# mLSTM heads: the sample part of the denominators read ahead of unit 4's update, the prompt part behind the sums of squares

## What is computed

```
den = inter * einsum('bhtk,bhk->bht', qc, n) + sum(S, axis=-1)
h = num / maximum(abs(den), exp(-m_t))[..., None]
C_new = scale * C + einsum('bhsk,bhsv->bhkv', kw, vc)
n_new = scale * n + sum(kw, axis=2)
...
h = h * rsqrt(mean(h * h, axis=-1) + EPS)
```

## Time and profile before

| what | us |
|---|---|
| median of 3 runs | 1970.97 |
| lowest and highest | 1969.07, 1975.01 |
| the profiled execution | 1968.61 |
| its span | 1966.9 |
| PE busy | 1897.9 (96%) |
| DVE busy | 714.5 (36%) |
| ACT busy | 720.9 (37%) |
| POOL busy | 820.2 (42%) |

### The profile page before, as it was taken

One profiled execution on the slowest core, in us unless ns is written; L12 is line 12 of the kernel. 1 busy time (PEld: TensorE's weight loads), 2 busy tenths in 40 slices (PEclk: granted clock), 3 DMA queues, 4 the chain that ended last, 5 costly groups with the idle time before them and its releaser, 6 DMA issues.

```text
span 1966.9 us, 35914 instructions
## 1 busy us (share of the span) xinstructions
PE 1897.9 (96%) x13701; PEld 1755.9 (89%) x13701; DVE 714.5 (36%) x844; ACT 720.9 (37%) x1054; POOL 820.2 (42%) x683
## 2 busy tenths in 40 slices
PE   6999999999999999899999999999999999999997
PEld 6999999999999999898554654999999999999996
DVE  5687742111111122576756567222121111111213
ACT  3567743322222235434432432432443322222342
POOL 4242564453544544563110100543655535534442
PEclk7999999999999999999999999999999999999998
DMA  3232232223222223322478578322222222222222
GB/s 108 82 86 76 80 105 75 86 81 85 81 80 85 80 81 74 79 86 86 162 240 301 191 243 281 120 82 73 82 87 83 83 82 84 80 83 78 86 75 70
DMA packets 187147, 209.70 MB, mean 107 GB/s; under 512 B 24475, under 2 KB 150051, under 8 KB 186991
## 3 DMA queue, kind: packets, MB, share of 16 engines
q1 hardware_dynamic: 186394, 207.67, 33.8%
q10 hardware_dynamic: 648, 0.59, 0.1%
HBM read 167.57 MB, written 40.64 MB: 106 GB/s over the span
## 4 chain that ended last, share of the span: by engine, by line
PE 81%; issue 6%; DVE 5%; POOL 4%; ACT 3%; DMA 1%; ACTq 0%; POOLq 0%; DVEq 0%
PE ps L2145 68%; POOL W_LO L641 2%; PE ps L2434 2%; PE ps L2471 2%; PE ps L2373 2%; PE ps L2412 1%; POOL SQUARE_SUM L649 1%; PE ps L2489 1%; PE ps L2307 1%; PE ps L2422 1%; DVE H_PAD L1664 1%; DVE C_HALVES L1956 1%; DVE K_T L1827 1%; PE ps L2445 0%; DMA ML_IN_ROWS<-in_state_mlstm_conv_dram 0%
## 5 line engine op out<-in xcount | busy, mean ns | idle before, releaser
L641 POOL TENSOR_TENSOR W_LO<-W_RAW,W_HI 128x512 fp32r<-128x512 f32 x464 | 611.3, 1327 | 664.7 <-ACT W_HI L956 664.4
L956 ACT ACTIVATE W_HI<-W_RAW 128x512 fp32r<-128x512 f32 x484 | 297.8, 628 | 704.3 <-PE ps L2145 698.4
L2145 PE MATMUL ps<-A_HI,W_HI 128*128 128x288 f32 x2304 | 497.2, 298 | 15.1 <-POOL W_LO L641 6.6
L2145 PE MATMUL ps<-A_LO,W_HI 128*128 128x288 f32 x2304 | 494.7, 296 | 0.0
L2145 PE MATMUL ps<-A_HI,W_LO 128*128 128x288 f32 x2304 | 494.4, 296 | 0.0
L2145 PEld LDWEIGHTS ps<-A_HI,W_HI 128*128 128x128 f32 x2304 | 373.0, 190 | 18.0 <-issue 13.9
L2145 PEld LDWEIGHTS ps<-A_LO,W_HI 128*128 128x128 f32 x2304 | 373.0, 190 | 0.0
L2145 PEld LDWEIGHTS ps<-A_HI,W_LO 128*128 128x128 f32 x2304 | 372.6, 189 | 0.0
L2145 PE MATMUL ps<-G_HI,W_HI 128*128 128x288 f32 x768 | 164.7, 296 | 0.5 <-DVEq L1742 0.5
L2145 PE MATMUL ps<-G_LO,W_HI 128*128 128x288 f32 x768 | 164.5, 296 | 0.0
L2145 PE MATMUL ps<-G_HI,W_LO 128*128 128x288 f32 x768 | 164.4, 296 | 0.0
(11 more groups left out here) (368 smaller groups left out, 2333.2 us busy)
## 6 DMA issues: line engine op xcount, KB each, us to landing
W_RAW<-in_ffn_w_up_dram SPq DMA_DIRECT2D x176, 256.0 KB, 2.8
C_HALVES<-in_state_mlstm_C_dram SPq DMA_DIRECT2D x64, 512.0 KB, 4.9
out_ml_C_s_dram<-C_HALVES SPq DMA_DIRECT2D x64, 512.0 KB, 5.2
W_RAW<-in_ffn_w_down_dram SPq DMA_DIRECT2D x88, 256.0 KB, 2.7
W_RAW<-in_ml_w_in_dram SPq DMA_DIRECT2D x64, 256.0 KB, 2.8
W_RAW<-in_rg_w_in_dram SPq DMA_DIRECT2D x48, 256.0 KB, 2.8
W_RAW<-in_ple_w_gate_dram SPq DMA_DIRECT2D x32, 256.0 KB, 2.7
W_RAW<-in_ml_w_out_dram SPq DMA_DIRECT2D x32, 256.0 KB, 2.8
```

The costliest lines, as they stand in the source:

```text
L641: pool.tensor_tensor(W_LO[:, s], W_RAW[:, s], W_HI[:, s].bitcast(F32), ALU.subtract).then_inc(lo_ready, 1)
L956: act.activation(W_HI[:, s], W_RAW[:, s], ACT.Copy).then_inc(hi_ready, 1)
L2145: ins = pe.matmul(ps[:, 4 * s + 2 * m + h, 0:HALF_T], a[:, w, k, wc], x[:, h * HALF_T:h * HALF_T + HALF_T], start=i == 0 and k == 0 and q ...
```

## The change

`denominators` is split in two functions. The samples' part is called between update 3 and update 4, and the prompt's part where `denominators` was, behind `add_squares`. Each function waits at its end for its own last instruction. No instruction is added, left out or altered.

```diff
-            def denominators(h):
-
-                bank = at(h, "den")
-                if h == 0:
-                    dve.wait_ge(rows_spread, 16)
-                dve.wait_ge(piece_done, DONE[h, "den"])
-                link(dve.scalar_tensor_tensor(DEN[:, 0:SEQ], ps[:, bank, :], -1.0, EXP_NEG_M[:, 0:SEQ], ALU.mult, ALU.max))
-                dve.tensor_tensor(DEN[:, 0:SEQ], ps[:, bank, :], DEN[:, 0:SEQ], ALU.max).then_inc(bank_freed[bank], 1)
-                dbank, bank = bank, at(h, "ds")
+            def sample_denominators(h):
+
+                bank = at(h, "ds")
                 dve.wait_ge(piece_done, DONE[h, "ds"])
                 link(dve.scalar_tensor_tensor(DEN[:, SEQ:T], ps[:, bank, 0:N_STOK], -1.0, rows_of[h % 2][:, 1, :], ALU.mult, ALU.max))
                 dve.tensor_tensor(DEN[:, SEQ:T], ps[:, bank, 0:N_STOK], DEN[:, SEQ:T], ALU.max)
...
                 dve.wait_ge(bank_freed[bank], FREED[h, "ds", bank])
-                dve.wait_ge(bank_freed[dbank], FREED[h, "den", dbank])
+
+            def prompt_denominators(h):
+
+                bank = at(h, "den")
+                if h == 0:
+                    dve.wait_ge(rows_spread, 16)
+                dve.wait_ge(piece_done, DONE[h, "den"])
+                link(dve.scalar_tensor_tensor(DEN[:, 0:SEQ], ps[:, bank, :], -1.0, EXP_NEG_M[:, 0:SEQ], ALU.mult, ALU.max))
+                dve.tensor_tensor(DEN[:, 0:SEQ], ps[:, bank, :], DEN[:, 0:SEQ], ALU.max).then_inc(bank_freed[bank], 1)
+                dve.wait_ge(bank_freed[bank], FREED[h, "den", bank])
...
                 update(h, 3)
+                sample_denominators(h)
                 update(h, 4)
                 add_squares(h, Q_T[:, :, 0:SEQ], squares_p, sums_p)
-                denominators(h)
+                prompt_denominators(h)
                 update(h, 5)
```

## The result

The changed kernel is slower: a median of 1979.2 us over 20 runs, against 1969.03 us of the kernel before over 20 runs, a ratio of 1.0045 (95% interval 1.0025 to 1.0064). The forecast was 1961.5 us, in a range of 1956 to 1967. What strikes first is the spread. The kernel before ran from 1965.6 to 1975.5 us, the changed one from 1961.8 to 1988.7. Its two fastest executions, both 1961.8 us, are where the forecast was; half of all are above 1979. The profiled execution took 1979.06 us.

What follows compares the result with a forecast made beforehand. PE was taken as the bound, with `cp1` waiting 1.9 us a head for line 1989 and then running at half clock. 3.58 us a head, cut by load landings to 9.4 in all, gave 1961.5 us, range 1956.0 to 1967.0.

Steps and rivals of the forecast that it cites:

- The gain of head 3: End of head 3: its 3.1 us pass into the first slab's wait, as the last stores move with unit 7.
- the landings: Ahead of unit 7: it starts when its last half-unit load lands, limiting the gain to 1.5, 2.1, 2.7 and 3.1 us.
- These loads don't come earlier: Sample-state loads for unit 7: held by a chain of stores from updates 3 and 4, with DMA engines full.
- the sum: Four heads' gains, old start of unit 7 less its load's landing: 9.4 us off the span and the median.
- What hangs on the new wait: PE at unit 7: waits 0.5 to 2.1 us; clock loss taken as zero, upper bound 1.61 us a head.
- Rival 4: Behind unit 7: clock falls and stays down; with 8 us of half clock a head, 1977.6 us; chance 0.04.
- Rival 2: At unit 7: clock falls there instead, giving back 6.4 us, 1968.0 us (1964.8 in two heads only); chance 0.14.
- Rivals 1: Ahead of unit 7: loads don't hold it, transfers may pack better; gain 14.3 us, 1956.7 us; chance 0.14.
- 3: Change from head 3 to the slabs: head 3's gain lost, last stores held in queue; 1964.7 us; chance 0.14.
- 5: At `cp1`: a second condition nearly as late, so the change frees nothing; 1971 us; chance 0.04.

Runs made afterwards that it cites:

- e11: The changed kernel itself, run once more beside others on the same chip: 1982.0 us median of 12, ratio 1.0053 to the kernel before.
- e1: The kernel before with two added ScalarE copies of cp2, making PE idle about 1.9 us ahead of unit 7: 2018.8 us, ratio 1.0214.
- e8: The kernel before with one added ScalarE copy of cp2, a wait of about 1.3 us ahead of unit 7: 1975.2 us, ratio 1.0042.
- e4: The changed kernel with cp3's matmuls in one run behind cn and the samples' numerators behind them: 1962.6 us, ratio 0.9964.
- e7: The changed kernel with cn moved ahead of unit 7, cp3 in one run behind unit 7, then the numerators: 1966.3 us, ratio 0.9971.
- e3: The changed kernel with the first two of cp3's four row blocks moved ahead of unit 7, into its wait: 1964.2 us, ratio 0.997.
- e10: The changed kernel with cn and cp3's first row block moved ahead of unit 7, the rest in turns with numerators: 1958.8 us, ratio 0.9944.
- e12: The changed kernel with cp3's first row block moved ahead of unit 7 and cn left behind it: 1973.9 us, ratio 1.0026.
- e6: The kernel before with cp3 in one run behind cn, then the numerators, and no wait added: 1977.7 us, ratio 1.004.

## Why the prediction was wrong

*What held.* The samples' part fits DVE's idle time, update 4 keeps its place, and `cp1` starts behind unit 5 at full clock, as worked out (3.70 us). PE then waits for a load ahead of unit 7, as worked out, 0.5 to 1.9 us a head; it also waits 0.2 to 0.7 us ahead of unit 6, which the prediction did not have. The gain of head 3 passed into the slabs: PE's wait there is 3.21 us, as it was in the earlier trace rows, though the half clock behind it lasted longer, which costs 1.7 us.

*The first term that was mis-sized: the landings.* "These loads don't come earlier" was right; that they come no later was an unsaid part of the sum. Line 530 for half 15 of heads 1 and 2 after, to be read against the earlier trace rows:

```profile
L530 SPq DMA_DIRECT2D C_HALVES<-in_state_mlstm_C_dram x1: 380/380/380, 1067.8 to 1067.8; - x1
DMA to landing us min/median/max: 5.8/5.8/5.8
...
L530 SPq DMA_DIRECT2D C_HALVES<-in_state_mlstm_C_dram x1: 380/380/380, 1151.8 to 1151.8; - x1
DMA to landing us min/median/max: 5.5/5.5/5.5
```

Counted from each head's unit 4 (1055.35 and 1139.34), they land after 18.2 and 18.0 us; before it was 17.6 and 17.0. Unit 7 came 1.7, 1.3, 1.6 and 2.3 us earlier in the four heads, 6.9 us together where the sum had 9.4. In the profile of e11, the same kernel, it is 2.8, 2.9, 1.3 and 1.5, 8.5 together; so the landings move by more than a microsecond from head to head, and the term is smaller than 9.4 in both. What delays the chain of loads and stores was not tested.

*The step that failed: "What hangs on the new wait".* I took zero for the clock behind unit 7, with an upper bound of 1.61 us a head. Both the choice and the bound were wrong. The bound was taken from `cp1`, where eight large matmuls in a row follow a fall and it ends while they run. Behind unit 7 the large matmuls come in pairs among small ones, the fall lasts into the next head's projections, and its price is 10.1 us in the profile after and 11.6 in e1. The row that I let decide against a fall, the 2.7 us wait behind which the clock was 1.00, was one draw. The same place in the profile after, with half clock behind it from 939 to 943:

```profile
938.74 5.37 PE L2377 MATMUL ps<-Q_T,K_T 128*128 128x512 f32 x8 [2.67 <-DVE I_ROW L1847]
```

All 14 profiles have this wait, and in 10 of them these eight matmuls ran in part at half clock (4.9 to 5.4 us instead of 3.67). The fall behind `cp1`'s wait was a draw too, as e8 shows, so the 1.61 us a head that the sum takes for it are not lost in every execution of before.

*The rivals.* Rival 4 named the mechanism, a clock that falls at unit 7 and stays down, worked out its point of decision (4.7 us of half clock a head) and gave it a chance of 0.04, with the words that nothing in the trace shows so long a fall. The trace could not show it: it had no idle time at that place. What it did show was that PE's clock can fall in these heads, since it fell in all four behind 1.9 us, and that the fall ended while eight large matmuls ran, which do not stand behind unit 7 in one run. Those two rows together deserved a chance several times as large. Rival 2, with its price from `cp1`, was the same error in another coat. Rivals 1, 3 and 5 didn't come in.

*The range* was the four heads' gain with small corrections of both signs. A term that can cost 10 us in each of four heads, and does so at random, needed 1990 as its upper end.

## What to carry to other kernels

An idle time of TensorE that is moved costs what its new place makes of it. Ask what TensorE runs right behind the new wait: here eight large matmuls in a row brought a fallen clock back within 4 to 8 us, and a tail of small ones with large pairs among them kept it down to its end. If a wait has to stay, put independent work into it. Leave large matmuls among the small ones: they did not bring a fallen clock back, but a clock that was up was lost less often. With the large ones all ahead of the small ones it was lost among the small ones in 7 of 16 heads (e4 to e7), with two pairs among them in 2 of 4 (e3), with three in none of 8 (e10, e12). These are counts from one profile each. Where a kernel's times spread more than its neighbour's, read the granted clock of a few executions before the waits.

## What the runs showed of the hardware

- TensorE stayed at half clock for 23 us while its records show it busy 100% of the time (the changed kernel, 1076 to 1099), and for 26 us in e1, with small matmuls and four pairs of large ones in that time. The Trainium skill (TensorE: Matmul & The Clock Gate, What's actually happening) says that the throttled state is the default and that activity releases it. That fits what cp3 in one run did in e4; it also says that the gate goes by how busy the engine has been, and by busy time in the records these 23 us don't fit.
- It fell without any idle time, with 100% of busy time on both sides, amid small matmuls (e6 in head 1 at 1088, 3 us behind the last large one; e3 at 1005, 1.5 us behind a large pair). What in the mix decides was not isolated.
- The same program, in the same place, falls in one execution and not in the next: unit 7 of head 2 fell in one profile of the changed kernel (behind 2.05 us) and not in the other (behind 1.75), and its times go from 1961.8 to 1988.7 us. A single profile of such a kernel is one draw.
